# A streaming encoder step: scores of two heads in turn, selection by pairs of tiles, attention weights multiplied on GpSimd

## The reference

```python
logits = jnp.einsum('bqhd,bsd->bqsh', qi_b, ki)                   # indexer, 8 heads of 64
score = jnp.einsum('bqsh,bqh->bqs', jax.nn.relu(logits), wi_b)
score = jnp.where(admissible[None], score, -jnp.inf)              # chunks of 64 keys
_, idx = lax.top_k(score, top_k)                                  # 256 of the prompt's, 136 of the decode keys
k_sel, v_sel = gather(k, idx), gather(v, idx)
s = jnp.einsum('bqhgd,bqkhd->bqhgk', q_b, k_sel) * (HEAD_DIM ** -0.5)
p = jax.nn.softmax(jnp.where(valid, s, -jnp.inf), axis=-1)
out = jnp.einsum('bqhgk,bqkhd->bqhgd', p, v_sel)                  # 8 query heads, 2 kv heads, 64 wide
```

## Time and profile before

| | |
|---|---|
| median of 3 runs | 2713.3 us |
| profiled execution | 2712.45 us |
| its span, first to last instruction | 2710.5 us |
| mean granted TensorE clock | 0.958 |
| TensorE busy | 2553.4 us (94%) |
| GpSimd busy | 1362.5 us (50%) |
| VectorE busy | 995.9 us (37%) |
| ScalarE busy | 944.0 us (35%) |

### The profile page before, as it was taken

One profiled execution on the slowest core, in us unless ns is written; L12 is line 12 of the kernel. 1 busy time (PEld: TensorE's weight loads), 2 busy tenths in 40 slices (PEclk: granted clock), 3 DMA queues, 4 the chain that ended last, 5 costly groups with the idle time before them and its releaser, 6 DMA issues.

```text
span 2710.5 us, 40319 instructions
## 1 busy us (share of the span) xinstructions
PE 2553.4 (94%) x16301; PEld 2270.4 (84%) x16301; DVE 995.9 (37%) x1941; ACT 944.0 (35%) x1608; POOL 1362.5 (50%) x833
## 2 busy tenths in 40 slices
PE   8999998987999998897989899999999898999997
PEld 7888888776999998894489888888657888999997
DVE  1000006046710006038463588888654636000004
ACT  4333333323233232227434343333353333333230
POOL 3777565442666655341052567666302516666562
PEclk9999999998999999897799999999798999999999
DMA  4444432433233322333122223333401212433331
GB/s 139 121 119 114 154 94 67 107 99 129 86 94 90 90 71 64 104 86 113 56 63 62 64 76 103 110 94 95 150 1 59 59 39 63 128 115 94 94 92 59
DMA packets 420110, 245.07 MB, mean 90 GB/s; under 512 B 22817, under 2 KB 410977, under 8 KB 418657
## 3 DMA queue, kind: packets, MB, share of 16 engines
q1 hardware_dynamic: 389088, 195.65, 25.5%
q10 hardware_dynamic: 26480, 23.21, 2.8%
q0 software_dynamic: 4368, 23.73, 2.4%
HBM read 218.79 MB, written 21.74 MB: 89 GB/s over the span
## 4 chain that ended last, share of the span: by engine, by line
PE 75%; DVE 10%; DVEq 6%; issue 3%; ACT 2%; DMA 1%; POOL 1%; ACTq 1%; POOLq 0%; SPq 0%
PE LIN L645 63%; DVEq L1426 5%; DVE M L1423 5%; PE LIN L902 3%; PE TR L915 2%; PE TR L929 2%; DVE Y L1519 1%; PE LIN L722 1%; PE TR L698 1%; DMA spill_cl<-YCL 1%; DVE Y L1514 1%; PE LIN L884 1%; POOL WL L1754 1%; DVEq L1422 1%; PE TR L846 0%
## 5 line engine op out<-in xcount | busy, mean ns | idle before, releaser
L1754 POOL TENSOR_TENSOR WL<-WRAW,WH 128x1024 fp32r<-128x1024 f32 (+1 forms) x378 | 886.8, 2349 | 497.6 <-ACT WH L972 490.9
L645 PE MATMUL LIN<-XH,WH 128*128 128x256 f32 (+4 forms) x3016 | 834.5, 321 | 55.2 <-DVE Y L1462 25.3
L645 PE MATMUL LIN<-XH,WL 128*128 128x256 f32 (+4 forms) x3016 | 826.3, 318 | 0.0
L645 PE MATMUL LIN<-XL,WH 128*128 128x256 f32 (+4 forms) x3016 | 825.1, 318 | 0.0
L645 PEld LDWEIGHTS LIN<-XH,WH 128*128 128x128 f32 (+1 forms) x3016 | 530.5, 191 | 95.7 <-issue 50.5
L645 PEld LDWEIGHTS LIN<-XL,WH 128*128 128x128 f32 (+1 forms) x3016 | 531.1, 191 | 35.2
L645 PEld LDWEIGHTS LIN<-XH,WL 128*128 128x128 f32 (+1 forms) x3016 | 528.3, 191 | 34.8
L645 PE MATMUL LIN<-HH,WH 128*128 128x256 f32 (+2 forms) x1632 | 465.3, 307 | 8.5 <-POOL HL L1826 6.8
L645 PE MATMUL LIN<-HL,WH 128*128 128x256 f32 (+2 forms) x1632 | 462.9, 306 | 0.0
L645 PE MATMUL LIN<-HH,WL 128*128 128x256 f32 (+2 forms) x1632 | 462.2, 305 | 0.0
L972 ACT ACTIVATE WH<-WRAW 128x1024 fp32r<-128x1024 f32 (+2 forms) x382 | 393.0, 1030 | 145.3 <-PE LIN L645 54.8
(11 more groups left out here) (191 smaller groups left out, 2165.2 us busy)
## 6 DMA issues: line engine op xcount, KB each, us to landing
WRAW<-in_ffn_gate SPq DMA_DIRECT2D x88, 512.0 KB, 3.8
WRAW<-in_ffn_up SPq DMA_DIRECT2D x88, 512.0 KB, 3.8
WRAW<-in_ffn_down SPq DMA_DIRECT2D x64, 512.0 KB, 3.9
WRAW<-in_w_mix_in SPq DMA_DIRECT2D x44, 512.0 KB, 3.8
WRAW<-in_ffn_down SPq DMA_DIRECT2D x32, 384.0 KB, 3.4
WRAW<-in_w_mix_out SPq DMA_DIRECT2D x16, 512.0 KB, 3.9
WRAW<-in_w_mem_q SPq DMA_DIRECT2D x16, 512.0 KB, 3.9
WRAW<-in_w_mem_o SPq DMA_DIRECT2D x16, 512.0 KB, 3.9
```

The costliest lines, as they stand in the source:

```text
L645: last = pe.matmul(LIN[0:pr.rows, pr.slot, out:out + w], wt[:, pr.tile % RING, c, 0:pr.rows], x[:, c, col:col + w], start=(c == 0 and wt i ...
L1754: pool.tensor_tensor(WL[:, n % RING, 0:nk, 0:width], WRAW[:, n % 2, 0:nk, 0:width], WH[:, n % RING, 0:nk, 0:width].bitcast(F32), ALU.subtr ...
```

## The change

Heads come in the order 0, 1, 2, 3. Scores are issued for two jobs at once, an even and an odd head, alternating between them for each piece of up to 512 keys; the pair waits for both peaks of the pair before. The selection takes two tiles in one loop. The multiplication by the reciprocal goes from VectorE to GpSimd, which waits for the reciprocal (`rr_ready`); before a reciprocal VectorE waits until GpSimd has used the one of two jobs before. GpSimd's loads go behind its eighth multiplication.

```diff
 def att_jobs(g):
     return [(t, col, rows, keys, kvg, hh) for t, col, rows, keys in att_tiles(g)
-            for kvg in range(2) for hh in (0, 2, 1, 3)]
+            for kvg in range(2) for hh in range(4)]
...
-        M8 = place("M8", [P, 8], F32, region(32))
+        M8 = place("M8", [P, 2, 8], F32, region(64))
...
-                    def scores(a):
-                        t, col, rows, keys, kvg, hh = jobs[a]
-                        h, lo = 4 * kvg + hh, 64 * (hh % 2)
-                        if a >= 2:
-                            pe.wait_ge(nm_ready, s0 + a - 1)
-                        same = (kvg == 0) == (lo == 0)
-                        kmat = (KSA if same else KSB) if rows == DEC else (KPA if same else KPB)
+                    def scores(p):
+
+                        t, col, rows, keys, kvg, hh = jobs[2 * p]
+                        if p:
+                            pe.wait_ge(nm_ready, s0 + 2 * p)
                         for k0 in range(0, keys, 512):
                             w = min(512, keys - k0)
-                            last = pe.matmul(LIN[0:rows, a % 2, k0:k0 + w],
-                                             (QA1 if g.sample else QA0)[lo:lo + 64, h // 2, col:col + rows],
-                                             kmat[lo:lo + 64, k0:k0 + w], start=True, stop=True)
-                        last.then_inc(s_done, 1)
+                            for odd in range(2):
+                                h, lo = 4 * kvg + hh + odd, 64 * odd
+                                same = (kvg == 0) == (lo == 0)
+                                kmat = (KSA if same else KSB) if rows == DEC else (KPA if same else KPB)
+                                mm = pe.matmul(LIN[0:rows, odd, k0:k0 + w],
+                                               (QA1 if g.sample else QA0)[lo:lo + 64, h // 2, col:col + rows],
+                                               kmat[lo:lo + 64, k0:k0 + w], start=True, stop=True)
+                                if k0 + w == keys:
+                                    mm.then_inc(s_done, 1)
...
                     scores(0)
-                    scores(1)
                     for a in range(len(jobs)):
-                        if a + 2 < len(jobs):
-                            scores(a + 2)
+                        if a % 2 == 0 and a + 2 < len(jobs):
+                            scores(a // 2 + 1)
                         if a % 4 == 0 and a:
                             values(a // 4 - 1)
                         turn(a)
...
-                for t, rows, keys, rounds in score_tiles(g):
-                    at_ = SCORE_AT[(g.index, t)]
-                    sc = SC[0:rows, at_:at_ + keys]
-                    with dve.Fori(0, rounds):
-                        dve.max(M8[0:rows, :], sc)
+                tiles = score_tiles(g)
+                for k in range(0, len(tiles), 2):
+                    pair = tiles[k:k + 2]
+                    keys_of = [SC[0:rows, SCORE_AT[(g.index, t)]:SCORE_AT[(g.index, t)] + keys] for t, rows, keys, _ in pair]
+                    with dve.Fori(0, pair[0][3]):
+                        for i, sc in enumerate(keys_of):
+                            dve.max(M8[0:pair[i][1], i, :], sc)
                         dve.drain()
-                        dve.match_replace(sc, M8[0:rows, :], sc, TAKEN)
+                        for i, sc in enumerate(keys_of):
+                            dve.match_replace(sc, M8[0:pair[i][1], i, :], sc, TAKEN)
                         dve.drain()
-                    dve.tensor_scalar(sc, sc, CUT, FAR, ALU.is_gt, ALU.mult)
+                    for sc in keys_of:
+                        dve.tensor_scalar(sc, sc, CUT, FAR, ALU.is_gt, ALU.mult)
...
                         dve.wait_ge(exp_done, s0 + a + 1)
-                        link(dve.reciprocal(RR[0:rows, q, 0:1], RS[0:rows, q, 0:1]))
-                        dve.tensor_scalar(PR[0:rows, a % 4, 0:keys], PR[0:rows, a % 4, 0:keys], RR[0:rows, q, 0:1], None, ALU.mult)                            .then_inc(p_ready, 1)
+                        if a >= 2:
+                            dve.wait_ge(p_ready, s0 + a - 1)
+                        dve.reciprocal(RR[0:rows, q, 0:1], RS[0:rows, q, 0:1]).then_inc(rr_ready, 1)
...
                     if g.sample:
                         move(spill_y[0][:, :, 0:HALF], Y[:, :, 0:HALF])
-                        all_moved()
-                    move(Y[:, :, 0:g.cols], spill_y[g.index][:, :, 0:g.cols])
-                    move(HH[:, 0:KC, 0:g.cols].bitcast(F32), spill_ch[g.index][:, :, 0:g.cols])
-                    move(HL[:, 0:KC, 0:g.cols].bitcast(F32), spill_cl[g.index][:, :, 0:g.cols])
+                    for a, (t, col, rows, keys, kvg, hh) in enumerate(att_jobs(g)):
+                        if a == 8:
+                            all_moved()
+                            move(Y[:, :, 0:g.cols], spill_y[g.index][:, :, 0:g.cols])
+                            move(HH[:, 0:KC, 0:g.cols].bitcast(F32), spill_ch[g.index][:, :, 0:g.cols])
+                            move(HL[:, 0:KC, 0:g.cols].bitcast(F32), spill_cl[g.index][:, :, 0:g.cols])
+                        pool.wait_ge(rr_ready, ATT_AT[g.index] + a + 1)
+                        pool.tensor_scalar(PR[0:rows, a % 4, 0:keys], PR[0:rows, a % 4, 0:keys], RR[0:rows, a % 2, 0:1],
+                                           None, ALU.mult).then_inc(p_ready, 1)
                     all_moved()
```

More of the change, by code:

```diff
@@ L536, in encoder_step @@
         pt_done, pt_read = sem("pt_done"), sem("pt_read")
+        rr_ready = sem("rr_ready")
         o_done, o_hi, o_lo = sem("o_done"), sem("o_hi"), sem("o_lo")
```

## The result

The changed kernel took 2751.8 us (median of 4 runs, 2748.24 to 2753.15), the kernel before on the same chip 2713.7: a ratio of 1.0141, 95% interval 1.0124 to 1.0159, so 38 us slower. The forecast was 2710.8 with a range of 2702 to 2728. It was wrong, and by more than its worst rival.

The account below looks back on a forecast made before the run. TensorE was taken to set the pace, with only the two attention segments (210 us) and a barrier movable. Group 0 -3.2, group 1 0, reloads +0.6, barrier -0.3: -2.9, rounded to -2.5 from 2713.3, giving 2710.8 us; range 2702 to 2728.

Parts of the forecast that it names:

- its worst rival: The slowest case priced, GpSimd's multiplication at the two-input pace: +25, 2738 us; chance 0.22.
- Multiplication on GpSimd: Multiplication by the reciprocal in the attention segments: 0.97 us on GpSimd at 896 keys, just fitting, so no wait added.
- The third rival: GpSimd's multiplication runs at the two-input pace, 2.1 us at 896 keys, holding the second turns: +25, 2738; chance 0.22.
- above about 1.0 us it decides: At 896 keys, GpSimd's multiplication holds a pair's second turn once it takes longer than about 1.0 us.
- Only A2 with B1: Paired score matmuls overlap only there: five passes at 1024 keys; saves 11.1 us in group 0, 24 in group 1.
- the first rival: The clock rises earlier in group 0 because pairs fill both row halves: 4 to 8 us gained, 2704; chance 0.20.
- fourth rival: The clock falls in group 1 through recurring turns and waits, some 16 us at half clock costing 8: 2719; chance 0.05.
- The selection: Top-k selection by pairs on VectorE: ends some 26 us earlier, but GpSimd's weight split holds the barrier: only -0.3 us.
- The copy wait: A pair's second turn waits for ScalarE's PT copy, 1.1 us at 896 keys: 16.5 us plus some 4 in decode rows.
- `out_lo` ahead of the reciprocal: On VectorE it waits for a value product and delays the next reciprocal: 7.9 us in group 0, some 2 in group 1.
- second rival: Score matmuls on different row halves don't overlap, so costs stay and little is saved: +24, 2737 us; chance 0.04.
- The reloads: Three DMA issues moved before job 8 in GpSimd's queue: 0.3 us each, 0.6 together, bounds 0 and 4.

Follow-up runs that it names:

- same_row_half: Like vector_multiplies, but heads in the old order 0, 2, 1, 3, so both heads of a pair lie on the same half of the rows: 2735.8 us.
- vector_multiplies: The changed kernel with the multiplication back on VectorE and GpSimd's loads back at the segment's head: 2692.8 us, ratio 0.993.
- low_part_later: Like vector_multiplies, but VectorE's `out_lo` comes behind the next job's multiplication, no longer ahead of that job's reciprocal: 2682.8 us, ratio 0.9895.
- orders_by_pair: low_part_later plus ScalarE's copy over 512 keys in two pieces, and VectorE's and ScalarE's lists ordered by pairs in group 0: 2676.1 us, ratio 0.9855.

## Why the prediction was wrong, step by step

**The step that failed is "Multiplication on GpSimd".** It said "I take the line of one input, since the affine select reads one operand too": 0.97 us at 896 keys, and so no wait of its own in the sum. Measured 2.52. The second turn of a pair then stood for 2.71 us, released by GpSimd, and the multiplication put back on VectorE makes the kernel 59 us faster (57 by the ratios). The upper bound of 2.1 was too low as well, because it was taken from the two-input rows as if one input could not be slower. The row that bounds an operation from above is not there if no row shows the operation. What makes it slower than the two-input operation no run shows. The third rival named the right mechanism and the right place. It had 0.22, and its price of 25 us was sized for 2.1. Its point, "above about 1.0 us it decides", is not shown: with 1.41 us it decided, and no run lies between that and 0.69.

**The pair of scores was mis-sized, on the other side.** "Only A2 with B1" can overlap, three passes for one chunk: measured, the two heads' matmuls run side by side from the first pass to the last, 1.92 us at 1024 keys instead of 2.34. The prediction cited the Trainium skill, "TensorEngine Tiling (Array Packing)", section "Theoretical Speedup", with the twofold, and priced it at some 11 us less. That figure was right here: 1.92 against 3.63 us on the same half of the rows. I had argued it away with an order of issue that no row supported.

**The sum without GpSimd.** It would have missed too: 2692.8 us, where the forecast was 2710.8 with 2702 as its lower end. The two errors have opposite signs, and the first hides the second in the total. With VectorE multiplying, the two segments shrank by 9.3 and 14.4 us, where the forecast had 3.2 and 0. Of the 20.5 between them, 11 are the passes above by the prediction's price. The clock gave a part of the rest: it rose some 17 us earlier in group 0 and 13 earlier in group 1. The work that it reached by that, and that ran at half clock before, took 13.5 and 12.5 us in the kernel before (1311.0 to 1324.5, and 1943.5 to 1956.0). A value product of 384 keys takes 2.83 us there at half clock and 1.52 at full, so as an estimate the clock is worth up to half of 26 us. Its own share was not isolated. This was the first rival (0.20). Its reason, that pairs fill both halves, is borne out by same_row_half, where the clock rises as late as before; it took full effect only once GpSimd's wait was gone.

**The falling clock**, fourth rival (0.05, in group 1), came true in the changed kernel, through GpSimd's wait and not the copy's. It has its part in the rival's 25 us becoming 57. How large a part was not separated from the wait itself.

**What held.** The selection is worth nothing, and GpSimd's split ends last before the barrier. The copy wait is 1.10 us at 896 keys (predicted 1.1). As a price it was too high, though: in every second pair VectorE's multiplication, queued behind a peak, ends at the same time, so cutting the copy for half of the jobs gave 5 us and not half of its 20. `out_lo` ahead of the reciprocal cost 10 us (predicted 7.9 and 2). The row halves do overlap (second rival, 0.04, refuted). The price on that rival was near: without the overlap 2737, and same_row_half, which is that case, took 2735.8. Some luck is in it, since that price held no change of the clock, and its mean in group 0 was 0.54 where it was 0.65 before. The reloads were not tried by themselves, but the changed kernel's trace has them: in group 0 their issues hold GpSimd from 1284.93 to 1287.4, and the first turn of the next tile waits 0.69 us for it; in group 1 that turn waits for nothing (predicted 0.6 together).

**The GPSIMD Engine Reference** of the Trainium skill, section "Engine selection", was the rule against this part. Its half on two inputs, some twice as slow as VectorE, pointed the right way; the half on one input ("roughly line-rate"), which the sum followed, does not hold for this operation: 2.52 us on GpSimd and 0.69 on VectorE, 3.7 times as long.

## What to carry to other kernels

Before a step moves to an idle engine, ask how long it takes there and how long the path has for it. An engine that is 50% busy is no slack if the step sits between two others that TensorE waits for: here each microsecond of it, at 896 keys, cost some 30 us over the two segments. When no row shows the operation on that engine, let the range reach past the slowest neighbour, and measure the one instruction first. And alternate matmuls of 64 rows between the two halves: that part alone was worth keeping (18 us against before), and the orders of the other engines' lists around it gave about as much again (17).

## What the runs showed of the hardware

- GpSimd's multiplication by a scalar for each partition takes some 2.5 ns a column and 0.3 us (602 ns at 128, 2842 at 1024), more than its operation on two full inputs (2400 at 1024). 32 partitions are no faster than 128: 1633 ns at 544 columns lies on the same line.
- Two fp32 matmuls with 64 rows on different halves start within 0.01 us of each other and take the time of one (a pair of 1024 keys 1.92 us, one head alone 1.91); on the same half they follow each other (3.63).
- The granted clock rose after 49 us of group 0's attention before, with a head's scores on one half and TensorE hardly idle, and again after 49 in same_row_half; after 32 in vector_multiplies, with scores on both halves; and after 22 and 15 in low_part_later and orders_by_pair, with TensorE's waits cut. In the changed kernel it swung between its two levels where waits of 1.8 to 3.3 us recurred.
